# Moving rotary half turns and key doublings from permutation products on TensorE to block moves by DMA

## What is computed

```
def rope(x, pos, theta):                 # first block: branches A and B
    half = d // 2
    x1, x2 = x[..., :half], x[..., half:]
    return concatenate([x1 * cos - x2 * sin, x2 * cos + x1 * sin], axis=-1)

aq = rope(aq, pos); ak = rope(ak, pos)   # A: 8 query heads, 2 key heads of 64
bq = concatenate([rope(bq[..., :half], row), rope(bq[..., half:], col)])
...
# retention (odd mixer): 4 heads of 128, q and k through the same rotation
# branches A and B and the window attention: 8 query heads share 2 key heads
```

## Time and profile before

| | us |
|---|---|
| median of 3 runs | 3694.53 |
| lowest, highest | 3689.34, 3697.13 |
| span of the profiled execution | 3687.2 |
| TensorE (PE) busy | 3521.7 |
| VectorE (DVE) busy | 1623.9 |
| ScalarE (ACT) busy | 1018.1 |
| GpSimd (POOL) busy | 2094.5 |

### The profile page before, as it was taken

The page is one execution under the profiler, slowest core; times in us unless marked ns, Lnnn a source line. Parts: engine busy times, 40 slices in busy tenths (PEclk is TensorE's granted clock), DMA queues, the critical chain, the costliest instruction groups (busy, mean ns, idle before and its releaser), DMA issues.

```text
span 3687.2 us, 45174 instructions
## 1 busy us (share of the span) xinstructions
PE 3521.7 (96%) x17597; PEld 2759.6 (75%) x17597; DVE 1623.9 (44%) x2473; ACT 1018.1 (28%) x1967; POOL 2094.5 (57%) x2150
## 2 busy tenths in 40 slices
PE   8999998999999999989998999998999999989998
PEld 6777777888777777778886676775888777668886
DVE  3564436755436553477554544334322233233222
ACT  2344224212223341332112454333211133221111
POOL 5444574777554446657674554443677644447665
PEclk9999999999999999999998999998999999989999
DMA  5121332665221213236642222221333322123332
GB/s 146 58 69 58 87 89 89 201 186 163 85 75 55 67 46 111 78 117 193 186 131 71 69 72 64 73 60 55 103 97 94 89 70 59 55 70 92 97 92 75
DMA packets 578940, 345.22 MB, mean 94 GB/s; under 512 B 16047, under 2 KB 562216, under 8 KB 578728
## 3 DMA queue, kind: packets, MB, share of 16 engines
q1 hardware_dynamic: 577432, 340.17, 31.6%
q10 hardware_dynamic: 1296, 2.16, 0.2%
HBM read 340.14 MB, written 2.14 MB: 93 GB/s over the span
## 4 chain that ended last, share of the span: by engine, by line
PE 87%; DVE 7%; ACT 3%; issue 1%; DMA 1%; POOL 0%; SPq 0%; POOLq 0%; DVEq 0%; ACTq 0%
PE gemm L228 24%; PE gemm L231 23%; PE gemm L234 23%; PE scores L321 6%; PE outs L321 6%; PE scores L1608 1%; PE gemm L276 1%; PE gemm L277 1%; PE gemm L278 1%; DMA w_raw<-in_w_in 1%; DVE tiles L1233 0%; DVE tiles L1701 0%; PE scores L2404 0%; DVE work L1597 0%; DVE tiles L1698 0%
## 5 line engine op out<-in xcount | busy, mean ns | idle before, releaser
L207 POOL CAST w_high<-w_raw 128x512 fp32r<-128x512 f32 (+1 forms) x1067 | 699.4, 655 | 1463.3 <-PE gemm L234 1148.9
L209 POOL TENSOR_TENSOR w_low<-w_raw,w_high 128x512 fp32r<-128x512 f32 (+1 forms) x1067 | 1392.0, 1305 | 85.5
L228 PE MATMUL gemm<-x_high,w_high 128*128 128x512 f32 x2584 | 715.4, 399 | 21.9 <-DVE x_low L1865 4.8
L231 PE MATMUL gemm<-x_low,w_high 128*128 128x512 f32 x2584 | 693.1, 390 | 0.0
L234 PE MATMUL gemm<-x_high,w_low 128*128 128x512 f32 x2584 | 692.4, 390 | 0.0
L228 PEld LDWEIGHTS gemm<-x_high,w_high 128*128 128x128 f32 x2584 | 474.4, 189 | 130.3 <-issue 18.4
L231 PEld LDWEIGHTS gemm<-x_low,w_high 128*128 128x128 f32 x2584 | 485.3, 188 | 104.9
L234 PEld LDWEIGHTS gemm<-x_high,w_low 128*128 128x128 f32 x2584 | 485.1, 188 | 102.9
L228 PE MATMUL gemm<-split_tiles,w_high 128*128 128x512 f32 (+1 forms) x1456 | 391.1, 389 | 8.2 <-DVE tiles L1698 2.6
L231 PE MATMUL gemm<-split_tiles,w_high 128*128 128x512 f32 (+1 forms) x1456 | 379.6, 381 | 0.0
L234 PE MATMUL gemm<-split_tiles,w_low 128*128 128x512 f32 (+1 forms) x1456 | 378.7, 380 | 0.0
(11 more groups left out here) (352 smaller groups left out, 3639.8 us busy)
## 6 DMA issues: line engine op xcount, KB each, us to landing
w_raw<-in_mlp_w SPq DMA_DIRECT2D x112, 512.0 KB, 4.0
w_raw<-in_mod_w SPq DMA_DIRECT2D x96, 512.0 KB, 3.7
w_raw<-in_w_in SPq DMA_DIRECT2D x88, 512.0 KB, 3.7
w_raw<-in_f_w_up SPq DMA_DIRECT2D x88, 512.0 KB, 5.0
w_raw<-in_e_w_in SPq DMA_DIRECT2D x48, 512.0 KB, 3.9
w_raw<-in_f_w_down SPq DMA_DIRECT2D x32, 512.0 KB, 4.2
w_raw<-in_o_w_in SPq DMA_DIRECT2D x30, 512.0 KB, 3.8
w_raw<-in_w_branch SPq DMA_DIRECT2D x48, 256.0 KB, 2.6
```

The costliest lines, as they stand in the source:

```text
L207: me.pool.tensor_copy(WH[:, h, 0:n], W32[:, s, c0:c0 + n]).then_inc(sem["w_rounded"], 1)
L209: me.pool.tensor_tensor(WL[:, h, 0:n], W32[:, s, c0:c0 + n], WH[:, h, 0:n].bitcast(F32), ALU.subtract).then_inc(sem["w_split"], 1)
L228: me.pe.matmul(o, WH[:, h, (k - k0) * cols:(k - k0 + 1) * cols], src(k)[0], start=begin and k == 0, stop=False)
L231: me.pe.matmul(o, WH[:, h, (k - k0) * cols:(k - k0 + 1) * cols], src(k)[1], start=False, stop=False)
```

## The change

The permutation matrices leave the table of constants (15 matrices become 10) and the sine tables get the sign of the half that they multiply. A turn is then a plain exchange of row blocks, and ScalarE begins it as DMAs from the temporary tile to a second tile: 4 of 32 rows in A, 8 of 16 rows in B, 2 of 64 rows in the odd mixer, 256 KB in all each time. A doubling is 4 DMAs of 64 rows, 128 KB each, straight to the key tiles, without ScalarE's copy. VectorE adds the second tile instead of the PSUM bank. In B the turn is split over two steps: `rope_out` at the step where `rope_turn` was, the addition one step later.

```diff
+        def turn_by_dma(me, dst, src, half):
+
+            name = f"turn_landed{me.turns % 2}"
+            me.turns += 1
+            landed = me.tick(name, 16 * (P // half))
+            if me.act:
+                for p0 in range(0, P, 2 * half):
+                    for to, come in ((p0, p0 + half), (p0 + half, p0)):
+                        me.act.dma_start(dst[to:to + half], src[come:come + half]).then_inc(sem[name], 16)
+            return name, landed
+
+        def double_by_dma(me, dst, src):
+
+            landed = me.tick("keys_landed", 64)
+            if me.act:
+                for g in range(2):
+                    for m in range(2):
+                        me.act.dma_start(dst[64 * m:64 * m + 64, g, :],
+                                         src[64 * g:64 * g + 64, :]).then_inc(sem["keys_landed"], 16)
+            return landed
...
-                        me.dve.wait_ge(sem["pe_step"], after)
+                        me.dve.wait_ge(sem[after[0]], after[1])
...
-            def rope_turn(rot, parts, dst, tmp, free, copied=None):
-
-                turned, kept = parts
-                ready = me.tick("pe_step")
-                if me.pe:
-                    me.pe.wait_ge(sem["dve_step"], max(turned, free))
-                    if copied is not None:
-                        me.pe.wait_ge(sem["act_step"], copied)
-                    mm(me, O[:, 1, :], M[rot], tmp).then_inc(sem["pe_step"], 1)
+            def rope_out(half, parts, tmp, moved, free):
+
+                if me.act:
+                    me.act.wait_ge(sem["dve_step"], max(parts[0], free))
+                return turn_by_dma(me, moved, tmp, half)
+
+            def rope_turn(parts, dst, moved, landed):
+
                 made = me.tick("dve_step")
                 if me.dve:
-                    me.dve.wait_ge(sem["dve_step"], kept)
-                    me.dve.wait_ge(sem["pe_step"], ready)
-                    me.dve.tensor_tensor(dst, dst, O[:, 1, :], ALU.add).then_inc(sem["dve_step"], 1)
-                return ready, made
+                    me.dve.wait_ge(sem["dve_step"], parts[1])
+                    me.dve.wait_ge(sem[landed[0]], landed[1])
+                    me.dve.tensor_tensor(dst, dst, moved, ALU.add).then_inc(sem["dve_step"], 1)
+                return made
...
+                turned_at[i] = rope_out(32, parts[i], T2[:, i % 2, :], T[:, 11 + i % 2, :], made_q.get(i - 2, 0))
-                turned_at[i], made_q[i] = rope_turn("rotA", parts[i], dst, T2[:, i % 2, :], made_q.get(i - 1, 0))
+                made_q[i] = rope_turn(parts[i], dst, T[:, 11 + i % 2, :], turned_at[i])
...
+            if me.act:
+                me.act.wait_ge(sem["dve_step"], made_q[4])
+            ak_landed = double_by_dma(me, Ak, T2[:, 2, :])
+            av_t = me.tick("pe_step")
             if me.pe:
-                me.pe.wait_ge(sem["dve_step"], made_q[4])
-                for g in range(2):
-                    last = mm(me, Q[:, 2 + g, :], M[f"dup{g}"], T2[:, 2, :])
-                last.then_inc(sem["pe_step"], 1)
                 me.pe.wait_ge(sem["act_step"], av_raw)
...
-                        me.pe.wait_ge(sem["act_step"], ak_made)
+                        me.pe.wait_ge(sem["keys_landed"], ak_landed)
+                        me.pe.wait_ge(sem["dve_step"], made_q[4])
...
-                        me.pe.wait_ge(sem["dve_step"], b_ready["q"])
-                        me.pe.wait_ge(sem["act_step"], b_ready["k"])
+                        me.pe.wait_ge(sem["dve_step"], max(b_ready["q"], b_ready["scale"]))
+                        me.pe.wait_ge(sem["keys_landed"], b_ready["k"])
...
             def before_unit(s):
 
                 if s == 0:
-                    bparts["rot"], b_ready["k1"] = rope_turn("rotB", bparts["k"], T[:, 22, :], T[:, 23, :], 0)
-                elif 2 <= s < 6:
+                    bparts["rot"] = rope_out(16, bparts["k"], T[:, 23, :], T[:, 8, :], 0)
+                elif s == 1:
+                    b_ready["k1"] = rope_turn(bparts["k"], T[:, 22, :], T[:, 8, :], bparts["rot"])
+                elif 3 <= s < 7:
+                    i = s - 3
+                    b_ready["q"] = rope_turn(bparts[i], Bq[:, i, :], T[:, 7 + i % 2, :], bparts["rot"])
+                if 2 <= s < 6:
                     i = s - 2
-                    bparts["rot"], b_ready["q"] = rope_turn("rotB", bparts[i], Bq[:, i, :], T[:, 23, :],
-                                                            o1_free["dve"], b_ready.get("k"))
+                    bparts["rot"] = rope_out(16, bparts[i], T[:, 23, :], T[:, 7 + i % 2, :], b_ready["q"] if i else b_ready["k1"])
...
-                elif s in (3, 4):
-                    g = s - 3
-                    doubled, kd = me.tick("pe_step"), me.tick("act_step")
-                    if me.pe:
-                        me.pe.wait_ge(sem["dve_step"], max(b_ready["k2"], b_ready["q"]))
-                        mm(me, O[:, 1, :], M[f"dup{g}"], T[:, 22, :]).then_inc(sem["pe_step"], 1)
+                elif s == 3:
                     if me.act:
-                        me.act.wait_ge(sem["pe_step"], doubled)
-                        me.act.activation(Bk[:, g, :], O[:, 1, :], ACT.Copy).then_inc(sem["act_step"], 1)
-                    b_ready["k"] = kd
+                        me.act.wait_ge(sem["dve_step"], b_ready["k2"])
+                    b_ready["k"] = double_by_dma(me, Bk, T[:, 22, :])
...
+            if me.act:
+                me.act.wait_ge(sem["act_step"], raw[0])
+            doubled = double_by_dma(me, T[:, 16:18, :], T[:, 4, :])
...
+                    if me.act:
+                        me.act.wait_ge(sem["dve_step"], max(spun, side["added"]))
+                    side["tmp"] = turn_by_dma(me, moved_tile(h), turn_tmp, 64)
...
+                if n < 2:
+                    made[h, n] = side["added"] = me.tick("dve_step")
+                    if me.dve:
+                        me.dve.wait_ge(sem["dve_step"], landed[h, n])
+                        me.dve.wait_ge(sem[side["tmp"][0]], side["tmp"][1])
+                        me.dve.tensor_tensor(home(h, n), home(h, n), moved_tile(h), ALU.add).then_inc(sem["dve_step"], 1)
+                    return
```

More of the change, by code:

```diff
@@ L45 @@
 LAM_INIT = 0.8 - 0.6 * math.exp(0.0)
-CONSTS = ["ident", "ones", "mean", "pair", "rotA", "rotB", "rotC", "dup0", "dup1", "tri", "flip",
+CONSTS = ["ident", "ones", "mean", "pair", "tri", "flip",
           "row0", "row1", "row2", "row3"]
@@ L54, in constants @@
          "pair": (i[:, None] // 64 == i[None] // 64) / 64.0, "tri": (i[:, None] <= i[None]) * 1.0, "flip": np.eye(P)[::-1]}
-    for name, half in (("rotA", 32), ("rotB", 16), ("rotC", 64)):
-        m = np.zeros((P, P))
-        for o in range(P):
-            if o % (2 * half) < half:
-                m[o + half, o] = -1.0
-            else:
-                m[o - half, o] = 1.0
-        c[name] = m
-    for g in range(2):
-        c[f"dup{g}"] = (i[:, None] == 64 * g + i[None] % 64) * 1.0
     for q in range(4):
@@ L74, in table @@
         ang = np.stack([where(p) * inv[p % d % half] for p in range(parts)]).astype(np.float32)
-        return np.cos(ang).astype(f), np.sin(ang).astype(f)
+        sign = np.where(np.arange(parts) % d < half, 1.0, -1.0).astype(f)
+        return np.cos(ang).astype(f), np.sin(ang).astype(f) * sign[:, None]
     row, col = np.floor(pos / 64).astype(f), (pos % 64).astype(f)
@@ L163, in __init__ @@
                 self.raw_free = [None] * WRING
-                self.loads, self.units = 0, 0
+                self.loads, self.units, self.turns = 0, 0, 0
                 self.bank_freed = [None, None]
@@ L2830, in odd @@
             landed, made = {}, {}
-            side = {"bank": O[:, 1, :], "free": None, "tmp": None}
+            side = {"bank": O[:, 1, :], "free": None, "tmp": None, "added": 0}
+            moved_tile = lambda h: (RF[:, 4, :], RF[:, 4, :], RF[:, 6, :], T2[:, 3, :])[h]
             def take_in(h, n, done, bank):
@@ L2859, in turn_in @@
                         me.pe.wait_ge(sem[free[0]], free[1])
-                    me.pe.wait_ge(sem["dve_step" if n < 2 else "act_step"], landed[h, n])
-                    if n < 2:
-                        mm(me, bank, M["rotC"], turn_tmp).then_inc(sem["pe_step"], 1)
-                    else:
-                        for b in range(NB):
-                            last = me.pe.transpose(bank[:, b * P:(b + 1) * P], home(h, n)[:, b * P:(b + 1) * P],
-                                                   M["ident"])
-                        last.then_inc(sem["pe_step"], 1)
-                if n < 2:
-                    side["tmp"] = spun
-                    made[h, n] = me.tick("dve_step")
-                    if me.dve:
-                        me.dve.wait_ge(sem["pe_step"], spun)
-                        me.dve.tensor_tensor(home(h, n), home(h, n), bank, ALU.add).then_inc(sem["dve_step"], 1)
-                    side["free"] = ("dve_step", made[h, n])
-                else:
```

(6 more changed lines are left out.)

28 lines of the change are left out of this document (10 added, 18 removed).

## The result

The changed kernel takes 3709.83 us (median of three runs, and the time of the profiled one, whose span is 3708.0), the kernel before 3694.17 in the same session: a ratio of 1.0043, 95% interval 1.0027 to 1.0058, that is 15.7 us slower. The forecast was 3681.8, range 3663 to 3700. The side was wrong, and the time lies outside the range.

A forecast was written before the change was run, and what follows sets the result against it. TensorE, busy 96% of the span, was taken to bound the kernel. Branch A -2 x 6.1, branch B +2 x 4.2 and odd mixer -8.9 gave -12.7 us, a median of 3681.8, range 3663 to 3700.

The forecast's parts named there:

- Price of a product, branch A: Branch A, first layers: a product costs 0.87 us, landings are covered, so 7 products or 6.1 us per layer go.
- Price of a block move: DMA moves: 0.33 us per issue and 2.0 for landing, so 4.3 us for eight moves, 3.0 for four.
- Branch B, steps 1 and 2: First layers: step 1's product is worth nothing, and step 2 waits for the turned key: costs 1.0 us per layer.
- Branch B, steps 3 to 8, the ring: First layers: one temporary tile makes each query take 11.8 us against about 8: +1.8, plus 1.4 for clock, per layer.
- Odd mixer: Window attention of the odd mixer, from start through loop to last turns: -8.9 us in all.
- The start: Odd mixer before the first scores: a copy, then four moves landing, plus 1.4 for the clock: +1.9 us.
- The loop's four turns: Odd mixer's window loop: four turns are free of waits, so their products go: -3.5 us.
- the last turns: Odd mixer, last two turns: waits and products go, 3.35 us each, -6.7 us.
- (2,0) and (2,1): Two turns ending the odd mixer's window loop, no unit behind them: -0.6 us for both.
- The slower case: Rival: branch B's ring at its upper bound, landing 8.3 instead of 4.3 us, +24: 3706 us, chance 0.13.
- The case of no change: Rival: moves land 1 to 3 us later than taken, each us costing 6: 3687 to 3700, chance 0.15.
- Issues of "over 0.5 us": Sign the forecast is wrong: move issues under 0.1 or over 0.5 us in ScalarE's queue, where 0.3 was expected.

The follow-up runs named there:

- only_a: Kernel before with only branch A of both first layers on DMA moves; branch B and odd mixer stay on TensorE: 3685.21 us, ratio 0.9967.
- blocks64: Changed kernel, but a turn in branch B exchanges halves of 64 rows in 2 moves instead of 16-row blocks in 8, same bytes: 3685.73 us.
- two_temps: Changed kernel with two temporary tiles in branch B instead of one, ScalarE still beginning the moves: 3708.87 us.
- by_sync: Changed kernel with every move begun by SyncE instead of ScalarE, three weight loads later in its program: 3684.71 us.
- sync_two: Changed kernel with SyncE beginning the moves, three weight loads later, and two temporary tiles in branch B: 3663.41 us, ratio 0.9915.

## Why the prediction was wrong

In the traces the forecast and the run lie 29.3 us apart (-12.7 against +16.6): 20.7 in the first layers (-3.8 against +16.9) and 8.6 in the odd mixer (-8.9 against -0.3).

- **Price of a product, branch A.** Right: 6.0 us per layer in the trace, 12.2 for both by only_a's ratio (10.9 by its medians), against 12.2 forecast.
- **Price of a block move.** This is the failed step. "I take 0.33 per issue": it is 0.61, as probed on both queues, so the eight moves of a turn take 7 x 0.61 + 2.1 = 6.4 us to land, not 4.3. I took the row nearest in engine, isolated DMAs, for a burst. A burst was at hand: the eight of L2652, whose landing I used as an upper bound, have their issue price in the same answer, 432 ns in the median, up to 580. It would have given 7 x 0.43 + 2.0 = 5.0 us, a part of the way:

```profile
L2652 SPq DMA_DIRECT2D tiles<-bias_rows x8: 432/432/580, 2592.3 to 2595.8; - x8
```

The Trainium skill, page "DMA: Bandwidth & Descriptors", section Issuing engines are not separate DMA queues, has the time to initiate a DMA as usually small relative to the DMA itself. The rows of this case differ: one issue is 0.61 us beside a landing of 2.1, eight in a row take 5.0, and the issuing engine was the bound.
- **Branch B, steps 1 and 2.** +1.0 forecast, 2.3 in the trace (scores of step 3 at 136.76, 25.9 behind those of step 0, before 23.6). Right in kind: the product was worth nothing (wait of 1.81 in place of 0.96), and the addition came late.
- **Branch B, steps 3 to 8, the ring.** +1.8 and +1.4 forecast, 11.3 in the trace. Part is the price: by my own rule (each us of landing costs 6) 2.1 us more make 12.6 of the 16.2 missing in the two layers. The rest is a link that I left out: "those are needed only one step later and are counted above" was said of ScalarE's copies, but the square of the next query, which VectorE's multiplication needs at once, stands behind the issues too, at step 4 behind twelve. blocks64 shows that the issues were the cause, two_temps that they acted through ScalarE's program and not through the landing, by_sync that the ring lay close behind, sync_two that little lay behind the two. The colder clock after the waits, which I put at 1.4, is in these numbers: in the whole stretch of B it made TensorE's work 5.6 us longer.
- **Odd mixer.** The loop's four turns are right: -3.5 forecast, and -4.3 found with the product of (2,0), 0.87, in it. So are the last turns: -6.7 forecast, -6.5 found. The start is not: +1.9 forecast, +5.1 found. Nor are (2,0) and (2,1): -0.6 forecast, +3.4 + 2.1 - 0.9 = +4.6 found. At these two places nothing covers a move, and the last landing took 4.7 and 4.9 us where I had 2.1 and 2.0; at (2,1) I also gave the clock behind the wait no price.
- **The rivals.** The slower case was there (3706, chance 0.13), at the place named, but for the wrong reason: a late landing. That its time is near the measured one is luck. Its weight rested on the earlier trace rows read only for landing. The case of no change put the eight moves of B at 2.1 us more, 3694. That is the size by which they were dearer, but it came from moves run one behind the other by the DMA engines, and in B the landings stayed at 2.0 in the median. Issues of "over 0.5 us" stood among the signs that would make the forecast wrong, and it was that sign.

## What to carry to other kernels

Beginning a DMA is work for the engine that begins it: price a burst of them from a burst in the trace, and count who stands behind it in that engine's program. Even where TensorE sets the pace, a product of 0.87 us is cheap beside eight issues of 0.61 on an engine whose next square is awaited. On an engine with nothing urgent (SyncE, a few loads later), and with a second temporary tile, the same moves were worth 31 us. When one fix gives little, look at who ends the wait now, for two limits of nearly equal length hide each other.

## What the runs showed of the hardware

Issue prices in a burst were 0.42 to 0.68 us on ScalarE's and SyncE's queues alike, some single ones up to 1.7, whether 16, 64 or 128 rows and from SBUF or HBM; isolated DMAs from HBM took 0.33 to 0.37, and the first SBUF move of a burst 0.51. A weight load took 0.37 alone and 0.58 behind a burst of moves. Moves of 32 to 128 KB landed in 2.1 us in the median, and in 4.7 and 4.9 at two places beside a weight load. SyncE carried 156 moves between the weight loads, at 5 to 6 us per turn of B, and in sync_two TensorE had no wait in B for a weight.
